# Where the compressed branch's softmax is finished among the attention items of layer 0

## The reference

```python
sc = jnp.einsum('bghqd,bgnd->bghqn', qc, kc) * scale          # kc: 15 compressed keys
pc = jax.nn.softmax(jnp.where(cmask, sc, NEG), axis=-1) * cmask
o_cmp = jnp.einsum('bghqn,bgnd->bghqd', pc, vc)
...
o = g[:, :, 0] * heads(o_cmp) + g[:, :, 1] * heads(o_slc) + g[:, :, 2] * heads(o_win)
```

## Time and profile before

| what | value |
|---|---|
| median of 3 runs | 752.9 us (751.93 to 753.07) |
| the profiled execution | 749.46 us |
| its span, first to last instruction | 747.7 us |
| mean granted TensorE clock | 0.996 |
| PE busy | 722.3 us, 97% of the span |
| DVE, ACT, POOL busy | 284.6, 200.8, 110.9 us |

### The profile page before, as it was taken

One profiled execution on the slowest core, in us unless ns is written; L12 is line 12 of the kernel. 1 busy time (PEld: TensorE's weight loads), 2 busy tenths in 40 slices (PEclk: granted clock), 3 DMA queues, 4 the chain that ended last, 5 costly groups with the idle time before them and its releaser, 6 DMA issues.

```text
span 747.7 us, 9007 instructions
## 1 busy us (share of the span) xinstructions
PE 722.3 (97%) x3693; PEld 388.5 (52%) x3693; DVE 284.6 (38%) x527; ACT 200.8 (27%) x459; POOL 110.9 (15%) x91
## 2 busy tenths in 40 slices
PE   8999989999999999999999999999999999999984
PEld 4877756775343444343347887656434434434331
DVE  4385676264212121121255785636321212112214
ACT  5343679332101110110033546513210011011001
POOL 0011368422000000000033231401200000000001
PEclk9999999999999999999999999999999999999998
DMA  9999900157999999999999964016799999999992
GB/s 328 291 380 419 387 1 1 57 195 300 361 430 430 429 427 426 427 427 421 422 389 387 409 260 179 36 57 237 295 366 429 427 429 426 427 430 427 421 419 103
DMA packets 42700, 245.06 MB, mean 328 GB/s; under 512 B 5920, under 2 KB 10144, under 8 KB 29344
## 3 DMA queue, kind: packets, MB, share of 16 engines
q1 hardware_dynamic: 42656, 244.43, 81.3%
HBM read 243.37 MB, written 1.05 MB: 327 GB/s over the span
## 4 chain that ended last, share of the span: by engine, by line
PE 80%; DMA 9%; DVE 6%; ACT 2%; issue 1%; POOL 1%; SPq 0%; DVEq 0%
PE ps L861 25%; PE ps L882 13%; DMA ring<-in_w_up 8%; PE ps L781 5%; PE ps L583 4%; PE ps L585 4%; PE ps L584 4%; PE ps L846 3%; PE ps L892 3%; PE ps L674 2%; PE ps L660 2%; PE ps L699 2%; DMA ring<-in_w_in 1%; PE ps L837 1%; PE ps L806 1%
## 5 line engine op out<-in xcount | busy, mean ns | idle before, releaser
L861 PE MATMUL ps<-ring,R 128*64 128x512 f32 x928 | 227.1, 595 | 0.0
L861 PEld LDWEIGHTS ps<-ring,R 128*64 128x64 f32 x928 | 70.2, 137 | 108.8 <-issue 107.2
L882 PE MATMUL ps<-ring,R 128*64 128x512 f32 x448 | 113.4, 595 | 0.6 <-issue 0.6
L1117 ACT ACTIVATE wh<-ps,small 128x512 fp32r<-128x512 f32 x32 | 22.0, 687 | 265.4 <-PE ps L882 263.9
L1453 DVE TENSOR_TENSOR wl_r<-ring,wh 128x512 fp32r<-128x512 f32 x72 | 55.7, 791 | 42.6 <-ACT wh L1095 42.2
L882 PEld LDWEIGHTS ps<-ring,R 128*64 128x64 f32 x448 | 35.0, 137 | 67.7 <-issue 65.1
L1677 DVE SCALAR_TENSOR_TENSOR wl_r<-ps,small,wh 128x512 fp32r<-128x512 f32 x32 | 24.0, 751 | 105.3 <-ACT wh L1117 104.6
L583 PE MATMUL ps<-wh,xh_r 128*128 128x512 f32 x144 | 57.7, 401 | 1.0 <-DVE wl_r L1453 0.9
L1095 ACT CAST wh<-ring 128x512 fp32r<-128x512 f32 x72 | 44.4, 623 | 49.3 <-PE ps L585 47.9
L1666 DVE TENSOR_TENSOR R<-R,ps 128x512 f32<-128x512 f32 x16 | 17.2, 1074 | 104.8 <-PE ps L861 104.8
L585 PE MATMUL ps<-wh,xl 128*128 128x512 f32 x144 | 56.2, 391 | 0.0
(11 more groups left out here) (223 smaller groups left out, 997.0 us busy)
## 6 DMA issues: line engine op xcount, KB each, us to landing
ring<-in_w_gate SPq DMA_DIRECT2D x28, 2048.0 KB, 18.2
ring<-in_w_up SPq DMA_DIRECT2D x22, 2048.0 KB, 18.5
ring<-in_w_down SPq DMA_DIRECT2D x22, 2048.0 KB, 20.8
ring<-in_w_in SPq DMA_DIRECT2D x21, 1024.0 KB, 14.3
ring<-in_w_out SPq DMA_DIRECT2D x8, 1024.0 KB, 14.8
R<-in_w_up SPq DMA_DIRECT2D x4, 2048.0 KB, 18.0
R<-in_w_down SPq DMA_DIRECT2D x4, 2048.0 KB, 19.5
ring<-in_w_gate SPq DMA_DIRECT2D x8, 1024.0 KB, 25.7
```

The source lines that it names most:

```text
L861: last = mm(ps[64 * e:64 * e + 64, to, :], xe[:, j, at + 64 * e:at + 64 * e + 64], slots[e][:, j * UNIT:(j + 1) * UNIT], start=(j == 0), s ...
L882: last = mm(ps[64 * e:64 * e + 64, 2 + w, :], hT[:, k, 64 * e:64 * e + 64], slots[e][:, at:at + UNIT], start=(k == 0), stop=(k == FJ - 1))
```

## The change

`compressed_scale` is cut in two. Its first instruction, the sums, stays where all of it stood (step 3, behind the factors of item 2), as `compressed_sums`. The rest, reciprocal, two products with the gates and the scaling of `Pc`, moves into step 4, behind the maximum of item 4 and ahead of the factors of item 3. On PE the four compressed transposes move from the end of step 4 (behind the transposes of item 2, ahead of the mask and the scores of item 5) to step 5, behind the scores of item 5 and ahead of the values of item 2. No instruction is added or removed.

```diff
@@ PE, attention(l)
                     if l == 0 and m == 1:
                         compressed_scores()
+                    if l == 0 and m == 5:
+                        compressed_probs_transposed()
                     if m >= 3:
                         times_v(l, m - 3)
                     if (2, 4)[l] <= m < n + 2:
                         transpose_probs(l, m - 2)
-                    if l == 0 and m == 4:
-                        compressed_probs_transposed()
@@ DVE
+            def compressed_sums():
+                dve.wait_ge(c_exp, 1)
+                step(nc.vector.tensor_reduce(csum, Pc.rearrange("p (h n) -> p h n", n=CS), AX.X, ALU.add))
+
             def compressed_scale():
-                dve.wait_ge(c_exp, 1)
                 p3 = Pc.rearrange("p (h n) -> p h n", n=CS)
-                step(nc.vector.tensor_reduce(csum, p3, AX.X, ALU.add))
                 step(nc.vector.reciprocal(csum, csum))
@@ DVE, the loop over m
                     if m < n:
                         attention_max(l, m)
+                    if l == 0 and m == 4:
+                        compressed_scale()
                     if 1 <= m <= n:
                         coefficients(l, m - 1)
...
                     if l == 0 and m == 3:
-                        compressed_scale()
+                        compressed_sums()
```

## The result

The changed kernel took 747.68 us at the median of four executions (746.71 to 747.8), the kernel before 752.45 (751.93 to 753.07): a ratio of 0.9943 with an interval from 0.9916 to 0.9971. It is faster, as forecast, but by 4.8 us where 2.4 were forecast, and 747.68 lies under the range (749.4 to 752.3). The profiled execution took 747.59 us with a span of 745.8, against 749.46 and 747.7: only 1.9 us less. So the two profiles and the two medians tell different amounts, and that is the first thing to explain.

What follows compares the result with a forecast made beforehand. PE was taken to bound the kernel through the attention: -2.67 us for the wait removed, +0.25 for a wait on ACT, 0 for the rest, -2.42 in sum; 752.9 - 2.4 = 750.5 us, range 749.4 to 752.3.

Steps and rivals of the forecast that it cites:

- The wait removed: PE ahead of item 1's values, waiting on a DVE copy queued behind the scaling: 2.67 us expected to go.
- the new wait on ACT: PE ahead of item 5's mask, waiting for ACT's exponentials of item 3: 0.25 us added.
- the four moved DVE instructions: Reciprocal, two products and scaling on DVE in step 4: 1.38 us expected, 3.17 at today's price.
- item 3's transposes: PE in step 5: start at 103.48 us without waiting, since POOL delivers at 103.45; today 105.90.
- the compressed transposes in their new place: Four PE transposes in step 5, start at 102.01 us without a wait and take 0.44 us.
- item 6's mask: PE's end point of the sum: starts at 105.27 instead of 107.69 us, -2.42, carried in full to the kernel's end.
- the base: Median before stood 3.4 us above the profiled execution; -2.4 applied to the median 752.9 gives 750.5 us.
- own figure on the profiled execution: Whole kernel: profiled 749.46 us less 2.42 gives 747.0, span 745.3.
- Rival 1: DVE scaling takes 1.64 us even without POOL; PE waits on POOL before item 3's transposes; -1.45, 751.5 us; chance 0.13.
- Rival 2: Nothing arrives at the kernel's end because transfers take the time back; 752.9 us; chance 0.12.
- Rival 3: Slower: item 3's factors come late behind a scaling held by POOL; loss 3.3, 756.2 us; chance 0.07 including unseen causes.

Runs made afterwards that it cites:

- e4: Kernel before with PE's part alone: compressed transposes moved behind item 5's scores, scaling left whole in step 3; 751.42 us, ratio 1.0002.
- e8: Kernel before once more, unchanged, for counts of clock falls; 751.67 us, ratio 1.0006.
- e1: Kernel before, unchanged; 750.32 us at the median of 12, ratio 0.9983.
- e5: Kernel before with its PE idle time filled by ten 128x512 matmuls nobody reads; 749.59 us, ratio 0.9984.
- e6: Changed kernel with item 6's mask written to PSUM six times in place of once; 750.35 us, ratio 0.9995.
- e7: Changed kernel with the moved scaling one place later on DVE, behind the factors of item 3; 751.03 us, ratio 0.9995.
- e10: Kernel before with its PE idle time filled by ten unread matmuls, repeated for counts; 749.68 us, ratio 0.9992.
- e9: Changed kernel once more, unchanged, for counts; 747.19 us at the median of ten, ratio 0.9969.

## Why the prediction was wrong

**The path was right.** The wait removed was 2.67 us as forecast; the new wait on ACT 0.16 where 0.25 was forecast; the four moved DVE instructions took 1.36 us (99.28 to 100.64) where 1.38 was; item 3's transposes started without a wait on POOL. (The prediction speaks of five DVE instructions that change places; four do, and its sum has four.) The term that was most off is the compressed transposes in their new place, 0.59 us (101.68 to 102.27) where 0.44 was taken from the old place; why is open. The other steps differ by less than 0.1 us each. Sum -2.25 against -2.42 at item 6's mask, and 746.6 against 749.0 in executions at 0.994 and over: -2.4.

**The step that failed is the base:** "The median of the runs stands 3.4 us above the profiled execution; I apply the difference to it". That took the 3.4 us for a constant that the change leaves alone. It is not: the profiled execution, with a mean clock of 0.996, is one of those with no fall but the last, and only 34 of the 113 later executions of the kernel before reach 0.994. The median of the first runs lies, by its time, among those at 0.990 and less (the clock of those runs is not known, so this is inferred from their times). The prediction's own figure on the profiled execution, 747.0, is only 0.7 below the measured median. The means over the executions of the table are 751.1 before and 747.7 after, -3.4 us: -2.4 on the path; the remaining -1.0 goes with the falls, as executions at 0.990 or less went from 41 of 113 to 2 of 23. The rest of the first -4.8, some 1.3 us, is how the four executions of before came out: all at 751.9 or more, as are 39 of the 113 later ones. If it is luck, it is rare luck: four independent draws would do it about one time in seventy. Whether something else held in those first runs is open.

**What makes the clock fall.** That the idle time brings a fall is shown for the place where it stood. Of the four profiles with the 2.67 us in place three have a fall that begins inside it (e4, e8) or at its very end (e1) and one has none; of the eight with the idle time filled, removed or moved none has a fall from 97 to 110 us, though in three of them (e5, e6, e7) the clock had fallen near 90 us. And filling it with work nobody reads (e5, e10) takes the executions at 0.990 or less from 41 of 113 to 2 of 24 with the path unchanged. What filling cannot tell apart is the end of the idle time from the ten wide matmuls themselves; the changed kernel, without them, has 2 of 23. So the forecast missed a second price of the wait: behind it PE's next work could run at 1.2 GHz. The Trainium skill names it in "TensorE: Matmul & The Clock Gate", section "HAM oscillation — how this bites in real kernels", there for waits on transfers that are longer than this one: pauses of TensorE let its clock fall, and the work behind them starts slow. The rows of e8 agree, for a shorter pause (L699 at 1.98 us); those of the earlier trace rows show the same pause without a fall.

**The rivals.** Rival 1 falls with L1523's 0.69 us, and e7 shows what made it 1.64. Rival 2 falls with e6 and e9, but not without a rest: in the one profile the waits for expert weights took 0.6 us back. Rival 3's condition, POOL at work beside the scaling, is what e7 made, though with item 3's factors ahead of the scaling: there the hold came about and cost the gain, by PE's wait for the scaled probabilities and not by late factors.

**Open.** Near 90 us the clock falls in some executions with and without the idle time (e1, e4, e5, e6 and e7 in their profiles), with PE busy: it begins between 89 and 92 us, during or just behind the narrow matmuls of the compressed scores (L726). It was in none of the profiles of the changed kernel, but e6 and e7 have that stretch unchanged from it, so the change is not seen to do anything about it. Why 2.76 us of idle time at 103 us in e7 brought no executions at 0.990 or less, and why e6 had three with no more idle time than the changed kernel, was not settled.

## What to carry to other kernels

When a median and a profiled execution of one kernel differ by more than the runs of either, ask what the profile has not shown before adding the difference to a forecast; the mean clock of every execution is a quick look. An idle time of TensorE costs itself and can cost, in some executions, a slow stretch behind it (e8, not e7), so taking it out can be worth more than its length. And where a DVE instruction reads two SBUF operands, look what POOL does at that time: moved by one place in the queue, the same four instructions took 1.36 or 3.86 us (e7, 101.92 to 105.78).

## What was not expected of the hardware

Executions of one program spread over 6 us (748.4 to 754.3 beside e1), and it goes with the mean granted clock: 749.0 at 0.994 and over, 753.3 at 0.990 and less. Falls to 1.2 GHz came also right behind stretches in which the rows show PE busy without a break (84.0 to 89.5 us in e1, 5.50 of 5.50). And two DVE instructions with two SBUF inputs, a product and the scaling, ended each only behind one POOL instruction (104.10 and 105.78 us in e7), where in the changed kernel, with POOL idle, neither was held.
